# Rounded weights and their remainders, interleaved word by word in one buffer

## The reference

```python
for i in range(DEPTH):                       # the first block
    mix = gated_deltanet(h, ...) if i % N_MIXERS == 0 else short_conv_mixer(h, ...)
    h = layer_norm(ALPHA * h + mix, ln_mix_g[i], ln_mix_b[i])
    h = layer_norm(ALPHA * h + conv_ffn(h, ffn_w_up[i], ffn_conv[i], ffn_w_down[i]),
                   ln_ffn_g[i], ln_ffn_b[i])

def swiglu(x, w1, w3, w2):                   # the MLP of the second block
    return (jax.nn.silu(x @ w1) * (x @ w3)) @ w2
x = x + jax.nn.sigmoid(x @ ple_w_gate[i] + ple_b_gate[i]) * (p[i] @ ple_w_proj[i])   # after each layer of the second block
```

## Time and profile before

| | |
|---|---|
| median of 3 runs | 1395.0 us (1394.32 to 1395.79) |
| span of the profiled execution, from first to last instruction | 1393.3 us |
| mean granted TensorE clock | 0.997 of 2.4 GHz |
| matmuls on record | 10540 |
| HBM read | 223.40 MB, 161 GB/s over the span |

### The profile page before, as it was taken

How to read it: one execution, slowest core, us unless ns; L and a number is a source line. 1 busy time by engine, 2 the same in 40 slices (tenths; PEclk the granted TensorE clock), 3 DMA queues, 4 the chain that set the end, 5 groups by cost and what they waited for, 6 DMA issues and landing times.

```text
span 1393.3 us, 29518 instructions
## 1 busy us (share of the span) xinstructions
PE 1374.7 (99%) x10540; PEld 1319.5 (95%) x10540; DVE 1002.1 (72%) x1587; ACT 956.7 (69%) x1661; POOL 403.3 (29%) x426
## 2 busy tenths in 40 slices
PE   9999999999999999999999999999999999999998
PEld 8899989999999999999999899889998989988998
DVE  7867776886548878875578868665488776866557
ACT  5633347766876577667877868568878797756866
POOL 3343002432203335322045027212034403521203
PEclk9999999999999999999999999999999999999999
DMA  6533215566564564565656135555645614655662
GB/s 209 170 117 91 84 31 178 159 190 199 178 198 154 181 196 136 181 211 167 211 156 194 59 123 177 190 190 169 209 148 156 213 49 152 199 192 187 191 192 94
DMA packets 63163, 225.69 MB, mean 162 GB/s; under 512 B 7008, under 2 KB 8416, under 8 KB 63072
## 3 DMA queue, kind: packets, MB, share of 16 engines
q1 hardware_dynamic: 62064, 221.47, 51.5%
q10 hardware_dynamic: 1008, 3.01, 0.6%
HBM read 223.40 MB, written 1.05 MB: 161 GB/s over the span
## 4 chain that ended last, share of the span: by engine, by line
PE 85%; DVE 8%; ACT 4%; issue 2%; DMA 1%; POOL 0%; SPq 0%; DVEq 0%; ACTq 0%; POOLq 0%
PE bank L458 18%; PE bank L459 18%; PE bank L478 11%; PE bank L645 7%; PE bank L585 7%; PE bank L648 4%; DVE w_lo L1946 2%; ACT w_hi L1260 1%; PE bank L506 1%; PE bank L520 1%; PE bank L494 1%; PE bank L453 1%; PE bank L454 1%; PE bank L455 1%; PE bank L649 1%
## 5 line engine op out<-in xcount | busy, mean ns | idle before, releaser
L1946 DVE TENSOR_TENSOR w_lo<-raw,w_hi 128x1024 fp32r<-128x1024 f32 x294 | 378.1, 1301 | 33.9 <-ACT w_hi L1260 26.5
L1260 ACT ACTIVATE w_hi<-raw 128x1024 fp32r<-128x1024 f32 x298 | 312.1, 1051 | 42.9 <-PE bank L585 17.3
L458 PE MATMUL bank<-x_hi,w_hi 128*128 128x262 f32 (+6 forms) x1144 | 287.7, 287 | 0.0
L459 PE MATMUL bank<-x_lo,w_hi 128*128 128x262 f32 (+6 forms) x1144 | 284.6, 284 | 0.0
L1944 DVE SCALAR_TENSOR_TENSOR w_lo<-raw,negmean,w_hi 128x1024 fp32r<-128x1024 f32 x120 | 158.4, 1321 | 140.4 <-ACT w_hi L1258 139.9
L458 PEld LDWEIGHTS bank<-x_hi,w_hi 128*128 128x128 f32 x1144 | 216.0, 189 | 1.0 <-issue 0.5
L459 PEld LDWEIGHTS bank<-x_lo,w_hi 128*128 128x128 f32 x1144 | 216.4, 189 | 0.3
L2846 POOL TENSOR_TENSOR a_lo<-av,a_hi 128x256 fp32r<-128x256 f32 (+1 forms) x88 | 79.7, 906 | 333.8 <-ACT a_hi L1520 149.5
L1258 ACT ACTIVATE w_hi<-raw,negmean 128x1024 fp32r<-128x1024 f32 x117 | 134.6, 1151 | 30.9 <-PE bank L585 25.8
L459 PE MATMUL bank<-a_lo,w_hi 128*128 (+2 forms) x640 | 155.8, 281 | 0.0
L458 PE MATMUL bank<-a_hi,w_hi 128*128 (+2 forms) x640 | 155.8, 281 | 0.0
(11 more groups left out here) (520 smaller groups left out, 2988.9 us busy)
## 6 DMA issues: line engine op xcount, KB each, us to landing
raw<-w SPq DMA_DIRECT2D x418, 512.0 KB, 3.8
h<-h SPq DMA_DIRECT2D x4, 272.0 KB, 4.9
out<-h SPq DMA_DIRECT2D x8, 128.0 KB, 1.9
T<-cs ACTq DMA_DIRECT2D x1, 960.0 KB, 6.1
con_b<-cb ACTq DMA_DIRECT2D x1, 712.0 KB, 5.7
con_g<-ca ACTq DMA_DIRECT2D x1, 421.5 KB, 6.1
p_raw<-pin ACTq DMA_DIRECT2D x1, 256.0 KB, 2.6
smx<-pin ACTq DMA_DIRECT2D x1, 256.0 KB, 6.0
```

Of the source, the lines that this page charges most:

```text
L458: pe.matmul(o, wh, xh, start=first, stop=False)
L459: pe.matmul(o, wh, xl, start=False, stop=False)
L1260: A(w_hi[:, slot, :], raw[:, slot, :], ACT.Copy).then_inc(S("hi_ready"), 1)
L1946: V.tensor_tensor(w_lo[:, slot, :], raw[:, slot, :], w_hi[:, slot, :].bitcast(F32), ALU.subtract).then_inc(S("lo_ready"), 1)
```

## The change

One buffer `w_both` takes the place of `w_hi` and `w_lo`: 4 slots of 1024 pairs of words. Word 0 of a pair is the rounded weight, word 1 its remainder, so either half is read and written with a step of 8 bytes. `w_hi(slot, cols, u)` and `w_lo(slot, cols, u)` are now functions that give the view. For the thirteen units in BY_TOKEN, whose weights are the moving operand, the view is another one of the same bytes: the 1024 rounded weights first, then the 1024 remainders, both contiguous. The memory used is the same. All other lines of the diff replace `w_hi[:, slot, c]` by `w_hi(slot, c)` and the like, in the matmuls, in the operations of ScalarE, VectorE and GpSimd that write the halves, and in the two memsets of the first unit. No instruction, wait or order changes.

```diff
+BY_TOKEN = set(range(U["m_sbv"], U["m_sbv"] + 4)) | {U["m_ukv"]} | set(range(U["f_v"], U["f_v"] + 8))
+
...
-        w_hi = sb("w_hi", [P, RING, D], F32R)
-        w_lo = sb("w_lo", [P, RING, D], F32R)
+        w_both = sb("w_both", [P, RING, D, 2], F32R)
+        w_apart = w_both[:, :, :, :].rearrange("p s c h -> p s (c h)").rearrange("p s (h c) -> p s h c", h=2)
...
+        def w_hi(slot, cols=slice(0, D), u=None):
+
+            return w_apart[:, slot, 0, cols] if u in BY_TOKEN else w_both[:, slot, cols, 0]
+
+        def w_lo(slot, cols=slice(0, D), u=None):
+
+            return w_apart[:, slot, 1, cols] if u in BY_TOKEN else w_both[:, slot, cols, 1]
...
-                        rounded(o, w_hi[:, slot, k * P:k * P + P], x[0][:, k, cols], x[1][:, k, cols], k == 0)
+                        rounded(o, w_hi(slot, slice(k * P, k * P + P)), x[0][:, k, cols], x[1][:, k, cols], k == 0)
...
-                            pe.matmul(banks[i][:, 0:512], xh[:, k, tk], w_hi[:, slot, wc], start=(k == 0), stop=False)
+                            pe.matmul(banks[i][:, 0:512], xh[:, k, tk], w_hi(slot, wc, s), start=(k == 0), stop=False)
...
-                    A(w_hi[:, slot, :], raw[:, slot, :], ACT.Copy).then_inc(S("hi_ready"), 1)
+                    A(w_hi(slot, u=s), raw[:, slot, :], ACT.Copy).then_inc(S("hi_ready"), 1)
...
-                    V.tensor_tensor(w_lo[:, slot, :], raw[:, slot, :], w_hi[:, slot, :].bitcast(F32), ALU.subtract).then_inc(S("lo_ready"), 1)
+                    V.tensor_tensor(w_lo(slot, u=s), raw[:, slot, :], w_hi(slot, u=s).bitcast(F32), ALU.subtract).then_inc(S("lo_ready"), 1)
```

More of the change, by code:

```diff
@@ L327, in ba_columns @@
         def ba_columns(t):
[L329 removed]
+            return t.rearrange("p (k g n) -> p k g n", k=KT, g=4)[:, :, :, 0:8]
         def ba_dense():
@@ L493, in remainders @@
                             pe.wait_ge(S("lo_ready"), u + 1)
-                        pe.matmul(acc[u % RING][:, 0:N - narrow * q], w_lo[:, u % RING, k * P:k * P + P], x[0][:, k, narrow * q:N], start=False, stop=False)
+                        pe.matmul(acc[u % RING][:, 0:N - narrow * q], w_lo(u % RING, slice(k * P, k * P + P)), x[0][:, k, narrow * q:N], start=False, stop=False)
                 for i, k in enumerate(order):
@@ L505, in first_pair @@
                         o = acc[u % RING][:, 0:N - narrow * q]
-                        mm = pe.matmul(o, w_hi[:, u % RING, c], x[0][:, k, narrow * q:N], start=(i == 0), stop=False)
+                        mm = pe.matmul(o, w_hi(u % RING, c), x[0][:, k, narrow * q:N], start=(i == 0), stop=False)
                         if i == q == 0 and owed[0]:
@@ L519, in first_pair @@
                     for q, u in enumerate((u0, u0 + 1)):
-                        mm = pe.matmul(acc[u % RING][:, 0:N - narrow * q], w_hi[:, u % RING, c], x[1][:, k, narrow * q:N], start=False, stop=(i == KT - 1))
+                        mm = pe.matmul(acc[u % RING][:, 0:N - narrow * q], w_hi(u % RING, c), x[1][:, k, narrow * q:N], start=False, stop=(i == KT - 1))
                         if i == KT - 1:
@@ L531, in pair_by_tile @@
                             start_unit(u, u)
-                        rounded(acc[u % RING][:, 0:N], w_hi[:, u % RING, c], x[0][:, k, 0:N], x[1][:, k, 0:N], k == 0)
+                        rounded(acc[u % RING][:, 0:N], w_hi(u % RING, c), x[0][:, k, 0:N], x[1][:, k, 0:N], k == 0)
                 for u in (u0, u0 + 1):
@@ L535, in pair_by_tile @@
                     for k in range(KT):
-                        mm = pe.matmul(acc[u % RING][:, 0:N], w_lo[:, u % RING, k * P:k * P + P], x[0][:, k, 0:N], start=False, stop=(k == KT - 1))
+                        mm = pe.matmul(acc[u % RING][:, 0:N], w_lo(u % RING, slice(k * P, k * P + P)), x[0][:, k, 0:N], start=False, stop=(k == KT - 1))
                     mm.then_inc(S("unit_done"), 1)
@@ L567, in parts @@
                     xh, xl = operand(k, N)
-                    return bank[m][:, 0:N], w_hi[:, s % RING, c], w_lo[:, s % RING, c], xh, xl
+                    return bank[m][:, 0:N], w_hi(s % RING, c), w_lo(s % RING, c), xh, xl
                 def ready(u, k):
@@ L668, in _ @@
                 pe.wait_ge(S("x_hi"), k // 2 + 1)
-                pe.matmul(ba, w_hi[:, ba_slot, k * P:k * P + P], x_hi[:, k, 0:L], start=(k == 0), stop=False)
-                pe.matmul(ba, w_lo[:, ba_slot, k * P:k * P + P], x_hi[:, k, 0:L], start=False, stop=False)
+                pe.matmul(ba, w_hi(ba_slot, slice(k * P, k * P + P)), x_hi[:, k, 0:L], start=(k == 0), stop=False)
+                pe.matmul(ba, w_lo(ba_slot, slice(k * P, k * P + P)), x_hi[:, k, 0:L], start=False, stop=False)
             for k in range(KT):
                 pe.wait_ge(S("x_ready"), 2 * (k // 2) + 2)
-                mm = pe.matmul(ba, w_hi[:, ba_slot, k * P:k * P + P], x_lo[:, k, 0:L], start=False, stop=(k == KT - 1))
+                mm = pe.matmul(ba, w_hi(ba_slot, slice(k * P, k * P + P)), x_lo[:, k, 0:L], start=False, stop=(k == KT - 1))
             mm.then_inc(S("unit_done"), 1)
@@ L830, in proj_part @@
                     c = slice(k * 512 + m * P, k * 512 + m * P + P)
-                    mm = three(o, w_hi[:, slot, c], w_lo[:, slot, c], p0_hi[:, k, :], p0_lo[:, k, :], k == 0, k == 1)
+                    mm = three(o, w_hi(slot, c), w_lo(slot, c), p0_hi[:, k, :], p0_lo[:, k, :], k == 0, k == 1)
                     if n % 8 == 7:
@@ L1001, in tokens @@
                             tk = slice(i * P, i * P + P)
-                            mm = pe.matmul(banks[i][:, 0:512], xh[:, k, tk], w_lo[:, slot, wc], start=False, stop=(k == tiles - 1))
+                            mm = pe.matmul(banks[i][:, 0:512], xh[:, k, tk], w_lo(slot, wc, s), start=False, stop=(k == tiles - 1))
                     mm.then_inc(S("unit_done"), 1)
@@ L1011, in four @@
                         c = slice(k * 512 + m * P, k * 512 + m * P + P)
-                        mm = pe.matmul(banks[m][:, 0:SEQ], w_hi[:, slot, c], xh[:, k, 0:SEQ], start=(k == 0), stop=False)
+                        mm = pe.matmul(banks[m][:, 0:SEQ], w_hi(slot, c), xh[:, k, 0:SEQ], start=(k == 0), stop=False)
                         if owed[0]:
@@ L1015, in four @@
                             owed[0] = 0
-                        pe.matmul(banks[m][:, 0:SEQ], w_hi[:, slot, c], xl[:, k, 0:SEQ], start=False, stop=False)
-                        mm = pe.matmul(banks[m][:, 0:SEQ], w_lo[:, slot, c], xh[:, k, 0:SEQ], start=False, stop=(k == 1))
+                        pe.matmul(banks[m][:, 0:SEQ], w_hi(slot, c), xl[:, k, 0:SEQ], start=False, stop=False)
+                        mm = pe.matmul(banks[m][:, 0:SEQ], w_lo(slot, c), xh[:, k, 0:SEQ], start=False, stop=(k == 1))
                 mm.then_inc(S("unit_done"), 1)
@@ L2899, in z_low @@
                 pool.wait_ge(S("lo_ready"), u)
-                G.tensor_tensor(w_lo[:, u % RING, :], raw[:, u % RING, :], w_hi[:, u % RING, :].bitcast(F32), ALU.subtract).then_inc(S("lo_ready"), 1)
+                G.tensor_tensor(w_lo(u % RING), raw[:, u % RING, :], w_hi(u % RING).bitcast(F32), ALU.subtract).then_inc(S("lo_ready"), 1)
             for i in (7, 8):
```

24 lines of the change are left out of this document (12 added, 12 removed).

## The result

The changed kernel takes 1405.8 us median against 1394.9 us (four runs of each): ratio 1.0076, 95% interval 1.0064 to 1.0088. It is slower by 0.8%, where 4.7% faster was forecast. The profiled execution has a span of 1403.9 us, 10.6 us above the one before.

The account below looks back on a forecast made before the run. TensorE was taken to bound the kernel: matmul count times 120.0 ns between starts. 85% of a best 78 us, 66 us, off the 1393.3 span gave 1327, median 1329 us; range 1306 to 1445, the forecast's own 1306 to 1365.

Parts of the forecast that it names:

- Reading 1: TensorE's weight matmuls: the 11 to 13 ns above their columns hang on addresses, not on the other engines.
- Reading 2: TensorE's weight loads: the excess is no fixed price of a load, whose own floor is 111 ns.
- The 111 ns of the earlier trace: Eight plain fp32 weight loads in 0.89 us under 128-column matmuls, taken as the load's own floor.
- Reading 3: TensorE's matmuls: excess depends on the moving operand's pace, 2 ns for plain fp32, 20 ns for 512 rounded columns.
- each crossing costs some ns: In the buffer, a rounded moving operand overtakes the half-pace load several times per load, each time costing some ns.
- The pair of the earlier trace: Two plain fp32 256-column matmuls beside 128-column loads: 215 ns each, against 233 for a 512-column rounded matmul.
- Part 1: Weight loads with a step of 8 bytes: best 78 us gained, worst 89 us lost, 66 us gain taken.
- Part 2: The thirteen units by token keep contiguous halves: 156 matmuls, nothing changes.
- Part 3: ScalarE, VectorE and GpSimd write the halves with a step: taken as 0, VectorE at most 0.8 us more each.
- Parts 4 and 5: Three VectorE writes of w_hi at 750 ns, 0 to 1 us; first unit's memsets, under 1 us; both taken as 0.
- The rule of read ports: TensorE has two independent read ports, so loading weights takes no bandwidth from the running matmul; the step would gain nothing.
- Rival A: Weight loads touch more places and each meeting holds up moving columns: slower, 1484 us or some 1440; chance 0.21.

Follow-up runs that it names:

- by_tile: Kernel before, but one buffer with rounded and remainder tiles alternating in contiguous 128-word blocks, tiles 1024 bytes apart: 1395.4 us, ratio 1.0001.
- load_step8: Kernel before, with only TensorE's 128-column weight loads reading at a step of 8 bytes, writers untouched: 1403.7 us, ratio 1.0060.
- move_step0: Kernel before, with the moving operand of every weight matmul one column repeated, loads contiguous: 1339.0 us, ratio 0.960.
- token_step8: Changed kernel with the thirteen units by token stepped too, so 156 matmuls have a moving operand with a step of 8 bytes: 1440.9 us, ratio 1.033.
- load_step0: Kernel before, with each 128-column weight load reading one word 128 times: 1378.9 us, ratio 0.988.
- short_loads: Kernel before, with low-half activation matmuls in panels and row stages loading 8 of 128 weight columns: 1390.1 us, ratio 0.997.
- move_twice: Kernel before, with the moving operand of every weight matmul taking each of its first columns twice in a row: 1341.7 us, ratio 0.961.
- write_step8: Kernel before, with ScalarE and VectorE writing the weight halves at a step of 8 bytes, loads contiguous: 1397.4 us, ratio 1.0016.

## Why the prediction was wrong, point by point

- **What bounds the kernel:** right. TensorE's spacing sets the time before and after, and 10.3 of 10.6 us are in it.
- **Reading 1 (it hangs on addresses):** the rows were right, the reading was loose. That durations differ by tile shows that addresses matter. It does not show that two streams meet. Compared matmul by matmul, the distances in by_tile follow those of the kernel before (correlation 0.93) although its weight tiles lie elsewhere, those of load_step8 follow the changed kernel's (0.90), and the changed kernel's hardly follow those before (0.29). The pattern goes with the step of the loads, and not with where the weights lie, as far as these runs move them (by_tile does so by multiples of 512 bytes).
- **Reading 2 (no fixed price of a load):** right: 112 ns come back with a moving operand that stands still. (The 111 ns of the earlier trace rows stood beside plain matmuls of 128 columns, 107 ns by themselves, so that row alone could not say which of the two set it; move_step0 gives 112 for the loads.)
- **Reading 3 (pace of the moving operand), and "each crossing costs some ns":** this is the step that failed. No row showed a crossing. The pair of the earlier trace rows differs in the pace of the moving operand against the load, and also in the pieces that it needs in a nanosecond; I took the first for the cause. What the runs showed in its place is a price for the moving operand's own pieces: twice as many, beside untouched loads, take 224 ns more (token_step8), and of the 8 ns above 112 a load of one single piece takes away only 2.5 (load_step0), one of 8 words only 1 (short_loads). Doubling the load's pace gave back none of it (load_step8). move_step0 and move_twice, at 112 ns, would fit either reading.
- **Part 1 (70 us gained from the spacing, 8 from the 512 columns):** it turned into 10 us lost and 0. The load's own floor rose from 112 to 118 ns, a term I had at 111 for either step. It is mostly covered by the 120 ns of the moving operand: where all tiles begin at multiples of 1024 bytes and the spacing is 120 throughout (yp, y), it costs nothing. Over the whole kernel the 1521 matmuls that stood below 118 ns rise from 115.7 to 120.6 ns in the mean, the 4468 of 118 to 121 ns rise from 119.6 to 121.1, and the 2572 longer ones fall from 124.1 to 122.7 (in by_tile the same three groups keep 116.0, 119.7 and 123.8). Lifting every matmul below 118 ns just to 118 would give 0.4 of the 1.2 ns, so the slower load alone does not account for it. The other 0.8 ns, a load with 64 pieces instead of 32 beside a moving operand at its limit, is of the kind of the 2.5 ns of load_step0, but no run isolates it: that part of the cause stays open.
- **Part 2 (units by token unchanged):** right, and it is worth 35 us: token_step8.
- **Part 3 (writers):** VectorE right, at 0. ScalarE wrong: 95 and 92 ns a unit, inside the bound, 2 us by write_step8. Parts 4 and 5, put at nothing: 5 ns on each of three operations, and memsets of 0.91 and 1.03 us where they took 0.91 and 0.95: right.
- **The rule of read ports:** the Trainium skill, TensorE: Matmul & The Clock Gate (Part 2), has the loads' reads take nothing from the running matmul's. short_loads and load_step0 put it nearly right: the loads take 1 to 2.5 ns. I had weighed it against the 233 ns of the 512 columns, which move_step0 traces to the moving operand.
- **Rival A** was nearest in sign and kind (more places touched by each load), at about an eighth of its price, and its sign of being wrong came: loads longer than 189 ns. It made every meeting cost the same, where a load's 6 ns are mostly hidden behind the moving operand's limit.
- **The range:** 1306 to 1445 holds the 1405.8, but only since the rivals were drawn into it; the forecast's own ends at 1365. That is no merit of the reading.

## What to carry to other kernels

Count the 16-byte pieces that each side of a matmul reads, not only its words: a piece takes about 1.8 ns here, so a rounded four-byte operand at a column a cycle is already a little over the limit, and a step of 8 bytes in the weights is the last that is nearly free; 16 bytes doubles the time (118 to 233 ns). When a busy engine runs some per cent above its arithmetic, let each of its operands stand still in turn before building on a theory of how they collide. Then put the other operand still alone, to see how much of the gain needs both. A pair of rows that differ in two things at once (here pace and pieces) is not a price for either.

## What I had not expected of the hardware

A rounded moving operand of 256 to 272 columns does not run at its 107 to 113 ns while it reads new columns: 120 ns in the mean, and 112 once it reads none, a gain of 4% of the whole kernel that no layout tried here reaches. A load of 128 words takes 112 ns contiguous, 118 with a step of 8 bytes and 233 with a step of 16. ScalarE pays 95 ns per 1024 words for writing with a step of 8 bytes, and VectorE, reading and writing with it, nothing.
